# Layer modulation computed in two halves, with four projection pieces begun as half sums, in a one-core decoder block

## The reference

```python
cs = silu(c)                                  # c: one vector of 1024
mod = cs @ w_cond[l] + b_cond[l]              # 1024 x 6144
sh1, sc1, gt1, sh2, sc2, gt2 = split(mod, 6)
h = layernorm(x) * (1 + sc1) + sh1
z = h @ w_in[l]                               # 1024 x 4608
q, k, v, gu, gv, ga, gg = split(z, [512, 1024, 1536, 2048, 2560, 3584])
attn = causal attention with ALiBi, 8 heads of 64, over 256 tokens
u = gelu(gu); vv = group_norm(gelu(gv)); sgu = u * (w_spatial(lower) @ vv + b_spatial)
merged = sigmoid(ga) * (attn @ w_attn_up) + sigmoid(gg) * (sgu @ w_gmlp_up)
x = layernorm(ALPHA * x + (1 + gt1) * (merged @ w_out)) * ln1_g + ln1_b
h = layernorm(x) * (1 + sc2) + sh2
```

## Time and profile before

| | |
|---|---|
| median of three runs | 930.67 us |
| profiled execution | 928.75 us |
| its span, first to last instruction | 927.0 us |
| TensorE busy | 780.8 us, 84% |
| VectorE busy | 607.6 us, 66% |
| GpSimd busy | 491.3 us, 53% |
| ScalarE busy | 193.2 us, 21% |
| mean DMA rate | 365 GB/s |

### The profile page before, as it was taken

One profiled execution on the slowest core, in us unless ns is written; L12 is line 12 of the kernel. 1 busy time (PEld: TensorE's weight loads), 2 busy tenths in 40 slices (PEclk: granted clock), 3 DMA queues, 4 the chain that ended last, 5 costly groups with the idle time before them and its releaser, 6 DMA issues.

```text
span 927.0 us, 8441 instructions
## 1 busy us (share of the span) xinstructions
PE 780.8 (84%) x2726; PEld 452.5 (49%) x2726; DVE 607.6 (66%) x1367; ACT 193.2 (21%) x492; POOL 491.3 (53%) x529
## 2 busy tenths in 40 slices
PE   5999999999977779796978869796977869696974
PEld 4876578778634345353534425352534435352322
DVE  6326587225779865759585756748585765888556
ACT  1012122204032312212121204212121312213111
POOL 1000000000577677777777676777677677777670
PEclk8699999999999799898989899897989899897987
DMA  9999985591699999999999999999999999999994
GB/s 347 365 375 338 335 302 218 190 310 46 243 407 409 409 409 409 409 409 409 410 409 409 410 409 400 407 408 410 367 411 409 410 409 407 409 392 408 408 409 161
DMA packets 112283, 338.48 MB, mean 365 GB/s; under 512 B 9184, under 2 KB 20976, under 8 KB 112112
## 3 DMA queue, kind: packets, MB, share of 16 engines
q0 software_dynamic: 73728, 268.47, 72.9%
q1 hardware_dynamic: 35936, 67.11, 20.3%
q10 hardware_dynamic: 2576, 2.37, 0.8%
HBM read 336.87 MB, written 1.05 MB: 365 GB/s over the span
## 4 chain that ended last, share of the span: by engine, by line
PE 35%; POOL 28%; DMA 14%; issue 11%; DVE 10%; ACT 1%; SPq 0%; DVEq 0%; POOLq 0%; ACTq 0%
POOL ring L362 28%; PE bank L1215 14%; DMA ring<-in_peer_u_dram,small 13%; PE bank L1027 11%; PE bank L1020 3%; DVE ring L867 3%; PE bank L1146 2%; DMA ring<-in_w_cond_dram 2%; PE bank L1160 1%; DVE ln L638 1%; PE h_ps L993 1%; DVE small L814 1%; DVE small L811 1%; DVE small L812 1%; DVE small L813 0%
## 5 line engine op out<-in xcount | busy, mean ns | idle before, releaser
L867 DVE CUSTOM_DVE_ANT_0 ring<-ring,h_ps 128x1024 f32<-128x1024 f32 x256 | 312.0, 1221 | 181.5 <-DMA ring<-in_peer_u_dram,small 171.6
L362 POOL DMA_INDIRECT ring<-in_peer_u_dram,small x256 | 246.8, 964 | 273.7 <-DVE small L848 193.4
L1215 PE MATMUL bank<-ring,small 128*128 128x512 f32 x512 | 258.7, 670 | 116.2 <-ACT small L549 116.2
L362 POOL DMA_INDIRECT ring<-in_peer_v_dram,small x256 | 240.5, 939 | 99.8 <-issue 64.4
L1215 PEld LDWEIGHTS bank<-ring,small 128*128 128x128 f32 x512 | 109.4, 217 | 256.0 <-issue 256.0
L1215 PE MATMUL bank<-ring,h_sb 128*128 128x512 f32 x500 | 220.1, 599 | 6.2 <-ACT h_sb L549 6.2
L1215 PEld LDWEIGHTS bank<-ring,h_sb 128*128 128x128 f32 x500 | 94.8, 192 | 121.5 <-issue 121.5
L1027 PE MATMUL bank<-hT,ring 128*128 128x256 f32 x448 | 101.5, 387 | 1.1 <-ACT hT L418 1.1
L1027 PEld LDWEIGHTS bank<-hT,ring 128*128 128x128 f32 x448 | 85.9, 194 | 15.9 <-issue 4.4
L1179 PEld LDWEIGHTS bank<-hT,wpq 128*128 128x128 f32 x512 | 59.6, 192 | 7.2 <-issue 7.2
L1179 PE MATMUL bank<-hT,wpq 128*128 128x128 f32 x512 | 59.8, 275 | 0.0
(11 more groups left out here) (187 smaller groups left out, 547.5 us busy)
## 6 DMA issues: line engine op xcount, KB each, us to landing
ring<-in_w_cond_dram SPq DMA_DIRECT2D x10, 2048.0 KB, 13.9
ring<-in_w_in_dram SPq DMA_DIRECT2D x8, 2048.0 KB, 12.7
wpq<-in_w_peer_q_dram SPq DMA_DIRECT2D x8, 1024.0 KB, 12.9
ring<-in_w_cond_dram SPq DMA_DIRECT2D x4, 1024.0 KB, 14.5
ring<-in_w_out_dram SPq DMA_DIRECT2D x2, 2048.0 KB, 10.4
ring<-in_peer_u_dram,small POOLq DMA_INDIRECT x256, 8.6
ring<-in_peer_v_dram,small POOLq DMA_INDIRECT x256, 8.6
ring<-in_w_in_dram SPq DMA_DIRECT2D x2, 1024.0 KB, 15.7
```

Source lines behind the costliest of these rows:

```text
L362: nc.gpsimd.indirect_dma_start(out=dst[e], out_offset=None, in_=table[0], in_offset=bass.IndirectOffsetOnAxis(ap=idx[:, k:k + 1], axis=0)) ...
L867: V.tensor_tensor_reduce(u_ring[e], u_ring[e], h_ps[:], 1.0, 0.0, ALU.mult, ALU.add, acol[:, g, e:e + 1]).then_inc(dots_done, 1)
L1215: last = T.matmul(bank[ACC_BANKS[t][m]][:], diag_of(p, g)[:, e, :], v_ring[e][:, m * BLK:(m + 1) * BLK], start=False, stop=end, skip_group ...
```

## The change

Channels 0 to 511 need only c0 and c2. The new order is c0, c2, c1, c3. After c0 and c2 half of `mod1` and half of `hT` are made. The first four pieces (q and k) get a bank each (0 to 3) and are made as two sums of four chunks (`half_piece`): pieces 0 and 1 first half before the columns of c1, piece 2 between c1 and c3, piece 3 behind c3, then the four second halves. TensorE takes no rows of c1 and c3 any more; VectorE sums all eight. in0 and in1 are loaded in halves by chunks, the second halves behind c3. The ring no longer rotates: a table gives each block's slot, condition blocks and projection blocks mostly having two slots each, and c4 and later blocks come later in the order. All six `turn_weights` stand behind v, and each total stands one weight block later: c4's behind v and not k, c8's behind piece 10 in the loop over heads, where VectorE also saves it (behind head 1).

```diff
--- before.py
+++ after.py
@@ -50,15 +50,19 @@
 FAR = -1.0e30
-STREAM = [("c", 0), ("c", 1), ("c", 2), ("c", 3), ("in", 0), ("in", 1), ("c", 4), ("in", 2), ("c", 5), ("c", 6),
-          ("in", 3), ("c", 7), ("in", 4), ("c", 8), ("in", 5), ("c", 9), ("in", 6), ("c", 10), ("in", 7), ("c", 11),
-          ("in", 8), ("ua", 0), ("ug", 0), ("o", 0), ("o", 1)]
-SLOT = {b: n % SLOTS for n, b in enumerate(STREAM)}
-TURN = {b: n // SLOTS for n, b in enumerate(STREAM)}
+PLACES = [(("c", 0), 0), (("c", 2), 1), (("in", 0), 2), (("in", 1), 3), (("c", 1), 0), (("c", 3), 1), (("in", 2), 0),
+          (("in", 3), 1), (("c", 4), 2), (("c", 5), 3), (("c", 6), 2), (("in", 4), 0), (("c", 7), 3), (("in", 5), 1),
+          (("c", 8), 2), (("in", 6), 0), (("c", 9), 3), (("in", 7), 1), (("c", 10), 2), (("in", 8), 0), (("c", 11), 3),
+          (("ug", 0), 2), (("ua", 0), 1), (("o", 0), 3), (("o", 1), 0)]
+STREAM = [b for b, _ in PLACES]
+SLOT = dict(PLACES)
+TURN = {b: sum(SLOT[e] == SLOT[b] for e in STREAM[:n]) for n, b in enumerate(STREAM)}
+BEFORE = {b: next((e for e in reversed(STREAM[:n]) if SLOT[e] == SLOT[b]), None) for n, b in enumerate(STREAM)}
+C_PLACE = {n: p for p, n in enumerate([0, 2, 1, 3, 4, 5, 6, 7, 8, 9, 10, 11])}
 IN_Q, IN_K, IN_V, IN_GU, IN_GV, IN_GA, IN_GG = 0, 1, 2, 3, 4, 5, 7
 PIECES = 18
-TE_ROWS = {0: 2, 1: 2, 2: 2, 3: 1}
+TE_ROWS = {0: 2, 1: 0, 2: 2, 3: 0}
 DVE_ROWS = (1, 3, 5)
 PE_ROWS = tuple(e for e in range(GROUP) if e not in DVE_ROWS)
 GT1, SH2, SC2, GT2 = range(4)
@@ -172,7 +176,7 @@
         bank = [ctx.enter_context(nc.psum_tensor(f"bank{i}", [P, BLK], F32)) for i in range(6)]
         h_ps = ctx.enter_context(nc.psum_tensor("h_ps", [P, D], F32))
         bank += [h_ps[:, 0:BLK], h_ps[:, BLK:D]]
-        PIECE_BANKS = (0, 1)
+        PIECE_BANKS = (0, 1, 2, 3) + 7 * (0, 1)
         SCORE_BANKS = (2, 3)
         TURN_BANK, GATE_BANK, ATTN_BANK, COND_BANK = 4, 5, 6, 7
         TURN1_BANKS, ATTN1_BANK = (6, 7), 0
@@ -180,7 +184,7 @@
         UP_BANKS = ((0, 1, 4, 5), (4, 5, 2, 3))
         OUT_BANKS = ((2, 3), (4, 5))
         XT_BANKS, HT_BANKS = (2, 3, 4, 5), ((6, 7), (4, 5))
-        WT_BANKS = (2, 3, 4, 5, 6, 2)
+        WT_BANKS = (4, 5, 6, 2, 3, 4)
         Q_BANK, S_BANK = 0, 1
         ACC_BANKS = ((2, 3), (4, 5))
@@ -271,15 +275,15 @@
                      "ug": w_gmlp_up[0].rearrange("(k p) n -> p k n", p=P)}
             sp.dma_start(x_sb[:], x[0].rearrange("(t p) d -> p t d", p=P)).then_inc(x_in, 16)
-            for n, b in enumerate(STREAM):
+            for b in STREAM:
                 kind, i = b
-                if n >= SLOTS:
-
-                    old, j = STREAM[n - SLOTS]
+                if BEFORE[b] is not None:
+
+                    old, j = BEFORE[b]
                     if old == "c":
-                        sp.wait_ge(cacc_ready, j + 1)
-                        if j in TE_ROWS:
-                            sp.wait_ge(cond_sum, j + 1)
+                        sp.wait_ge(cacc_ready, C_PLACE[j] + 1)
+                        if TE_ROWS.get(j):
+                            sp.wait_ge(cond_sum, C_PLACE[j] + 1)
                     elif old == "in":
                         sp.wait_ge(piece_ready, 2 * j + 2)
                     else:
@@ -289,14 +293,17 @@
                 else:
                     dst, src = slot(b).rearrange("p (k n) -> p k n", k=KC), w_of[kind][:, :, i * BLK:(i + 1) * BLK]
-                    if b in (("c", 2), ("c", 3)):
-                        sp.dma_start(dst[:, 0:KC // 2, :], src[:, 0:KC // 2, :]).then_inc(c_first[i], 16)
+                    early = c_first.get(i) if kind == "c" else in_first[i] if kind == "in" and i < 2 else None
+                    if early is not None:
+                        sp.dma_start(dst[:, 0:KC // 2, :], src[:, 0:KC // 2, :]).then_inc(early, 16)
                         dst, src = dst[:, KC // 2:KC, :], src[:, KC // 2:KC, :]
-                    if b == ("in", 0):
-                        sp.dma_start(dst[:, :, 0:SEQ], src[:, :, 0:SEQ]).then_inc(in0_first, 16)
-                        dst, src = dst[:, :, SEQ:BLK], src[:, :, SEQ:BLK]
-                    sp.dma_start(dst, src).then_inc(w_arrived[SLOT[b]], 16)
-                if b == ("c", 4):
+                    if early is None or kind == "c":
+                        sp.dma_start(dst, src).then_inc(w_arrived[SLOT[b]], 16)
+                    if b == ("c", 3):
+                        for n in range(2):
+                            later = slot(("in", n)).rearrange("p (k n) -> p k n", k=KC)[:, KC // 2:KC, :]
+                            sp.dma_start(later, w_of["in"][:, KC // 2:KC, n * BLK:(n + 1) * BLK]).then_inc(w_arrived[SLOT[("in", n)]], 16)
+                if b == ("c", 5):
                     sp.dma_start(cond[:].rearrange("p a n -> p (a n)"),
                                  b_cond[0:1, 2 * D:6 * D].broadcast_to([P, 4 * D])).then_inc(bcond_in[1], 16)
                 if b == ("c", 10):
@@ -411,8 +418,8 @@
             act.wait_ge(xT_ready, 1)
-            act.wait_ge(mod1_ready, 2)
             for r in (0, 2):
+                act.wait_ge(mod1_ready, 2 + r)
                 for m in range(2):
                     k = 2 * r + m
                     nc.scalar.activation(hT[:, k, :], bank[XT_BANKS[r]][:, m * SEQ:(m + 1) * SEQ], ACT.Identity,
@@ -465,11 +472,8 @@
             for n in range(2 * IN_GA):
                 piece(n)
-                if n == 3:
-                    save_wT(0)
-                    save_wT(1)
                 if n == 5:
-                    for m in range(2, 6):
+                    for m in range(6):
                         save_wT(m)
             act.wait_ge(gvar_ready, 1)
             nc.scalar.activation(gst[:, 2, :], gst[:, 1, :], ACT.Sqrt, bias=eps[:], scale=1.0 / HD).then_inc(gstd_ready, 1)
@@ -626,15 +630,16 @@
                     dve.wait_ge(c_first[n], 16)
                 else:
                     dve.wait_ge(w_arrived[SLOT[b]], 16 * (TURN[b] + 1))
-                if n >= 2:
-                    dve.wait_ge(cond_sum, n - 1)
+                place = C_PLACE[n]
+                if place >= 2:
+                    dve.wait_ge(cond_sum, place - 1)
                 w = slot(b).rearrange("p (k n) -> p k n", k=KC)
-                acc = cacc[:, n % 2, :]
+                acc = cacc[:, place % 2, :]
                 link(V.tensor_scalar(acc, w[:, 0, :], c_col[:, 2, 0:1], None, ALU.mult))
                 last_row = KC - 1 - TE_ROWS.get(n, 0)
                 for k in range(1, last_row + 1):
                     if n in c_first and k == KC // 2:
-                        dve.wait_ge(w_arrived[SLOT[b]], 16)
+                        dve.wait_ge(w_arrived[SLOT[b]], 16 * (TURN[b] + 1))
                     ins = V.scalar_tensor_tensor(out=acc, in0=w[:, k, :], scalar=c_col[:, 2, k:k + 1], in1=acc,
                                                  op0=ALU.mult, op1=ALU.add)
                     if k < last_row:
@@ -652,15 +657,15 @@
                 V.scalar_tensor_tensor(out=part, in0=bank[GT2_BANKS.get(n, COND_BANK)][:], scalar=one, in1=part,
                                        op0=ALU.add, op1=ALU.add).then_inc(cond_saved, 1)
-            for n in range(4):
-                cond_block(n)
-            dve.wait_ge(cond_sum, 4)
-            V.tensor_copy(mod1[:, 0, :], bank[COND_BANK][:, 0:KC]).then_inc(mod1_ready, 1)
-            V.tensor_scalar(mod1[:, 1, :], bank[COND_BANK][:, KC:2 * KC], 1.0, None, ALU.add).then_inc(mod1_ready, 1)
-            dve.wait_ge(mod1_ready, 2)
-
-            dve.wait_ge(xT_ready, 1)
             for r in (1, 3):
+                cond_block(r // 2)
+                cond_block(2 + r // 2)
+                dve.wait_ge(cond_sum, r + 1)
+                ks = slice(2 * r - 2, 2 * r + 2)
+                V.tensor_copy(mod1[:, 0, ks], bank[COND_BANK][:, ks]).then_inc(mod1_ready, 1)
+                V.tensor_scalar(mod1[:, 1, ks], bank[COND_BANK][:, KC + 2 * r - 2:KC + 2 * r + 2], 1.0, None, ALU.add).then_inc(mod1_ready, 1)
+                dve.wait_ge(mod1_ready, r + 1)
+                dve.wait_ge(xT_ready, 1)
                 for m in range(2):
                     k = 2 * r + m
                     V.tensor_scalar(hT[:, k, :], bank[XT_BANKS[r]][:, m * SEQ:(m + 1) * SEQ], mod1[:, 1, k:k + 1],
@@ -670,7 +675,6 @@
                 cond_block(n)
                 if n > 4:
                     cond_save(n - 1)
-            cond_save(8)
             def wide(v):
@@ -729,8 +733,8 @@
                     V.tensor_scalar(pj[t], pj[t], asum[:, 1, j, t:t + 1], None, ALU.mult).then_inc(probs_ready, 1)
                 if j in (0, 2, 4):
                     cond_block(9 + j // 2)
-                if j == 3:
-                    cond_save(9)
+                if j in (1, 3):
+                    cond_save(8 + j // 2)
                 if j == 5:
                     save_gate(0)
             save_gate(1)
@@ -969,21 +973,20 @@
                 b = ("c", n)
                 w = slot(b).rearrange("p (k n) -> p k n", k=KC)
```

(85 more changed lines are left out.)

## The result

The changed kernel took 922.5 us (four runs, 921.68 to 922.71) against 930.48 before: ratio 0.9921, 95% interval 0.9909 to 0.9934. Forecast were 924.3 us and 6.4 us less. The medians lie 7.98 us apart in the first comparison (the ratio makes it 7.35) and 6.36 in the second (929.46 and 923.10). The profiled executions are 928.75 and 922.54, their spans 927.0 and 920.8: 6.2 less.

What follows compares the result with a forecast made beforehand. TensorE was taken to bound from 33.56 to about 229 us, then the gathers, so earlier savings reach the end one for one. 7.7 gained less 1.3 is 6.4 us, off the 930.67 median: 924.3 us, range 921.8 to 927.8.

Steps and rivals of the forecast that it cites:

- Loads ahead: Start, SP's load queue: blocks land in queue order at 388 GB/s, c1 in at 24.8 and 27.5, c3 30.2 and 32.9.
- First half of the modulation: Start: after c0 and c2 only, the projection can start at 23.05, 10.5 us earlier than 33.56.
- Half sums: First four pieces: half sums run while VectorE sums c1 and c3; done at 55.8, not 63.46, 7.7 us gained.
- The same matmuls in another order: First pieces to head loop: transposes and a total move, sum zero; in4 lands 81 to 84, slack 4 to 6.
- Rival D: in4 behind b_cond takes 26.6 us to land: 96.2 against 87.7, 8.5 lost, 932.8 us; chance 0.03.
- ScalarE's hold: Six ScalarE loads behind the last modulated tile: issuing 38.8 to 52.5, cost nothing, cover 1.8 us before V.
- VectorE behind: Head loop: totals one block later start the group norm 4.75 us later; TensorE waits 0.6 twice, cost 1.3 us.
- A: Clock falls at each stop for column sums: 4.6 us lost, 928.9, or 926.6 with one fall; chance 0.08.
- B: c1 and c3 land late, from 31.6 and 36.6; pieces end at 62.4, 930.9 us, no change; chance 0.06.
- C: ScalarE held by its issues until 62.5, V starts at 64.0, 8.2 us late, 932.5; chance 0.06.
- E: Group norm's delay in the head loop costs nothing: 923.0 us; chance 0.05.

Runs made afterwards that it cites:

- c1_early: Changed kernel with c1 loaded ahead of in1's first half, not behind it: 922.32 us, 0.9929 of the kernel before.
- c3_early: Changed kernel with c1 and c3 both loaded ahead of in1's first half: 926.23 us, 0.9968 of the kernel before.
- again: The changed kernel itself, no edit, in more rounds: 0.9927 of the kernel before, six runs from 921.88 to 924.30 us.
- Columns_first: Changed kernel with all four condition blocks' column sums ahead of the first half piece: 936.12 us, 1.0066 of the kernel before.
- loads_late: Changed kernel with ScalarE's four small loads issued behind piece 3's save: four runs, 922.03 to 924.23 us, 0.9939 of the kernel before.
- norm_first: Changed kernel with c8's block behind head 0, c9's behind head 1, totals and saves moved along: 921.81 us, 0.9914 of the kernel before.
- all_four: norm_first and c3_early together, 28 dense products in front, c7's total behind piece 10: 919.7 to 924.0 us, 0.9920 of the kernel before.

## Why the prediction was right, and where its terms were off

1. *Loads ahead.* c1's second half and in0, in1 went by the queue. c3's first half was costed at 30.2 and came at about 31.6 (VectorE waits for it until 31.64); why it fell behind the queue's order isn't shown. c1_early and c3_early show that it set the end of VectorE's sums.
2. *First half of the modulation* at 23.05: measured 23.00. Right for that kind of run. That TensorE's rows and sums are hidden beside VectorE is wrong in the other kind (again: 25.97), which neither the trace before nor the prediction shows.
3. *Half sums.* 9.54 for the first two against 9.15 forecast, since the clock rose 4.8 us into them and not 4.1, the wait for c3 0.80 against 0.15; the pieces done at 56.12, not 55.8: 7.34 won, not 7.7. Columns_first shows that this step is the gain.
4. *The same matmuls in another order*: sum zero, confirmed by the stretches. But the slack of in4 was overrated. It was issued at 70.67 (forecast 69.6), behind c6 at 70.08, and took 16.2 to land where 11.4 to 14.4 were forecast:

```profile
ring<-in_w_cond_dram SPq DMA_DIRECT2D x1, 2048.0 KB, 11.3
ring<-in_w_in_dram SPq DMA_DIRECT2D x1, 2048.0 KB, 16.2
```

These are c6 and in4 of the changed kernel, from issue to landing. 70.67 + 16.2 is 86.9; TensorE takes it up at 88.0. 1.1 us of slack, not 4 to 6. Rival D was near.
5. *ScalarE's hold*: from 39.05 to 53.38, forecast 38.8 to 52.5; no wait of TensorE. loads_late confirms the zero.
6. *VectorE behind*: two waits of 0.46 and 0.49 where 0.6 and 0.6 were forecast; with smaller gaps beside them 1.46 given back, forecast 1.3. norm_first takes back 1.26 of it. The group norm starts 8.02 behind the end of gv (101.73 to 109.75), before 3.48 (109.94 to 113.42): 4.54 later, forecast 4.75.
7. *Rivals.* A didn't come in the changed kernel and did in all_four, at one stop. (Its price was summed too low: two stops with sums of 1.86 and 4.1 us of low clock behind each end the pieces at 61.3, not 60.4.) B is refuted by 23.00 and 31.64, C by 53.42, D by the row above, E by the two waits. The gather stage was a plain shift within its spread (687.45 against 687.77).

The terms of the sum held: 7.34 for 7.7 and 1.46 for 1.3, 5.88 for 6.4. That the spans make it 6.20 is luck, by 0.32 that lies within the gather stage's spread. The median came 1.8 under the 924.3, probably because the forecast started from three runs of the upper level (930.3 to 930.7) and all four runs after were of the lower.

The page rules named there: the clock rule of the Trainium skill (TensorE: Matmul & The Clock Gate, HAM oscillation — how this bites in real kernels), that groups with waits between them start at the low clock, is borne out by all_four's rows (0.50 behind the wait of 1.74), and not by c3_early's (1.00 behind 2.43) nor by the changed kernel's. The about 358 GB/s that the Trainium skill (DMA: Bandwidth & Descriptors, Specifications) gives as one core's share did not bound this core, which ran alone: 386 and 387 in the rows after.

## What to carry to other kernels

Work that needs only part of a long first sum can be started on that part: price it as the time of the dense engine's idle stretch, then look for the next load in line, since the order of loads is what it runs into. Moving a small total later on one engine moves every block behind it on the other; the price is read at the first place where the dense engine has to wait, not from the length of the chain. Put a margin at every load that a dense engine meets in its first microseconds: the waits of up to 0.8 us in the changed kernel cost only themselves, while one of 1.74 also cost the clock, and 1.7 us more with it, in one trace, and one of 2.43 did not in another.

## What had not been expected of the hardware

- The same program has two kinds of run, some 2 us apart, by whether 16 records of one column take 1.95 or 3.57 us at 14 us. With dense products from 2.5 us on no run of five was of the upper kind (all within 0.91 us, against 2.42 for six without).
- At the same place of the same order the clock fell at a stop with 1.74 us of idleness (all_four) and stayed up at one with 2.43 (c3_early).
- The granted clock in the profile can't be relied on ahead of its first change: 1.00 is given where the durations are those of the low clock.
